# Gated-linear-attention level scores as 64x64 blocks in two column strips of TensorE

## The reference

```
b     = cumsum(logf)                                  # log decay within the chunk
inter = (q * exp(b)) @ S
att   = einsum('tk,sk,tsk->ts', q, k, exp(b_t - b_s))  for s <= t
intra = att @ v
S_new = exp(b_last) * S + (k * exp(b_last - b)).T @ v
o     = inter + intra
```

## Time and profile before

| | |
|---|---|
| median of 3 runs | 1457.23 us (1452.88, 1457.23, 1464.98) |
| profiled execution | span 1456.3 us; the page gives no other time of its own |
| PE busy | 1295.0 us, 89% of the span |
| VectorE busy | 727.9 us, 50% |
| ScalarE busy | 411.9 us, 28% |
| POOL busy | 173.9 us, 12% |
| L906, score matmuls, x384 | 49.8 us busy |
| L786, masked copies, x48 | 35.1 us busy |

### The profile page before, as it was taken

One profiled execution on the slowest core, in us unless ns is written; L12 is line 12 of the kernel. 1 busy time (PEld: TensorE's weight loads), 2 busy tenths in 40 slices (PEclk: granted clock), 3 DMA queues, 4 the chain that ended last, 5 costly groups with the idle time before them and its releaser, 6 DMA issues. The chain is left out here.

```text
span 1456.3 us, 29957 instructions
## 1 busy us (share of the span) xinstructions
PE 1295.0 (89%) x11855; PEld 763.7 (52%) x11855; DVE 727.9 (50%) x1882; ACT 411.9 (28%) x1100; POOL 173.9 (12%) x247
## 2 busy tenths in 40 slices
PE   6999999999799999876999989868778699998897
PEld 3445565556356665444555545445554355755452
DVE  4435777768655311137353544477885565321123
ACT  3023444544111211124213121234546211121112
POOL 2002233332011000003021100100100001000002
PEclk9999999999899899997999999988999799799998
DMA  6150437223804899995465899899999622899935
GB/s 235 59 152 2 122 88 222 76 79 133 292 35 156 330 374 349 322 331 195 145 232 216 331 338 375 330 405 378 408 404 365 224 99 90 333 366 340 351 84 195
DMA packets 133902, 348.15 MB, mean 239 GB/s; under 512 B 22603, under 2 KB 52478, under 8 KB 125566
## 3 DMA queue, kind: packets, MB, share of 16 engines
q1 hardware_dynamic: 115378, 311.53, 59.8%
q10 hardware_dynamic: 13388, 16.82, 3.5%
q0 software_dynamic: 4992, 17.83, 3.3%
HBM read 302.61 MB, written 43.52 MB: 238 GB/s over the span
## 5 line engine op out<-in xcount | busy, mean ns | idle before, releaser
L409 PE MATMUL bank<-wring,xT 128*128 128x512 f32 x448 | 199.6, 600 | 0.0
L409 PEld LDWEIGHTS bank<-wring,xT 128*128 128x128 f32 x448 | 83.9, 192 | 100.0 <-issue 99.9
L1443 PE MATMUL bank<-wring,xT 128*128 128x512 f32 x256 | 120.2, 623 | 2.0 <-DVE xT L1363 2.0
L886 PE MATMUL bank<-xT,wring 128*128 128x512 f32 x256 | 115.0, 608 | 3.9 <-DVE hgrn_g L708 3.9
L2812 DVE STREAM_TRANSPOSE attn_k_pages<-attn_k_pages 128x1024 f32<-128x1024 f32 x64 | 77.6, 1232 | 38.9 <-DMA attn_k_pages<-cache_k 38.4
L886 PEld LDWEIGHTS bank<-xT,wring 128*128 128x128 f32 x256 | 49.2, 194 | 66.2 <-issue 60.6
L1443 PEld LDWEIGHTS bank<-wring,xT 128*128 128x128 f32 x256 | 49.7, 201 | 60.1 <-issue 60.0
L2812 DVE STREAM_TRANSPOSE wring<-wring 128x1024 f32<-128x1024 f32 x44 | 52.7, 1223 | 47.0 <-DMA wring<-cache_k 47.0
L786 DVE COPY_PREDICATED gla_att<-level_masks,bank 128x512 f32<-128x512 int32 x48 | 35.1, 731 | 70.4 <-PE bank L906 70.4
L2321 PE MATMUL bank<-xT,wring 128*128 128x512 f32 x128 | 56.9, 597 | 0.0
L906 PE MATMUL bank<-gla_qe,gla_ke 128*128 128x128 f32 x384 | 49.8, 285 | 0.0
(11 more groups left out here) (461 smaller groups left out, 2388.2 us busy)
## 6 DMA issues: line engine op xcount, KB each, us to landing
attn_k_pages<-cache_k SPq DMA_DIRECT2D x64, 512.0 KB, 7.4
wring<-cache_v SPq DMA_DIRECT2D x56, 512.0 KB, 7.8
wring<-cache_k SPq DMA_DIRECT2D x44, 512.0 KB, 7.2
moe_wd<-moe_w_down SPq DMA_DIRECT2D x20, 1024.0 KB, 13.8
attn_shared<-cache_v SPq DMA_DIRECT2D x40, 512.0 KB, 5.7
wring<-moe_w_gate SPq DMA_DIRECT2D x18, 1024.0 KB, 11.9
wring<-moe_w_up SPq DMA_DIRECT2D x18, 1024.0 KB, 14.8
wring<-a_w_in SPq DMA_DIRECT2D x16, 1024.0 KB, 10.7
```

The costliest lines, as they stand in the source:

```text
L409: last = nc.tensor.matmul(bank[:, :], xT[:, c, cols(t)], w[:, c, :], start=(c == 0), stop=(c == DC - 1))
L886: last = nc.tensor.matmul(bank[:, :], lhsT, k.xT[:, c, 0:SEQ], start=(c == 0), stop=(c == DC - 1))
L1443: last = nc.tensor.matmul(bank[:, :], k.xT[:, c, cols(t)], w[:, c, :], start=(c == 0), stop=(c == DC - 1))
```

## The change

- Scores of a level are formed as blocks of 64 keys by 64 queries. For levels 0 to 4 only the two diagonal blocks of each chunk matter: 8 matmuls with 64 stationary and 64 moving columns, key block n in PSUM partitions 64n to 64n+63, so that the two of a chunk stand in two column strips of TensorE. For level 5 only the block of lower keys and upper queries is formed: 4 matmuls, all in the first strip. A head has 44 score matmuls in place of 24.
- Two levels share a bank (level 0 and 1 in bank 3, 2 and 3 in bank 4, 4 and 5 in bank 3 again), and `att_done` is raised once per two levels. PE waits once: before level 4, for levels 0 and 1 to be taken.
- DVE copies levels 0 to 4 by mask into a compact tile `gla_diagonals` (64 columns a chunk), and level 5 by a plain copy into its quarter of A.
- ACT copies the compact tile into the diagonal quarters of A (`diagonals_out`, two copies of 64 partitions); PE waits for it before A times v.
- QE[i] and KE[i] of levels 1 to 5 are one tile (queries in the upper halves, keys in the lower), and nothing of it is cleared. POOL makes the 64-column masks in the setup, 2 copies.

```diff
--- before.py
+++ after.py
@@ -37,6 +37,7 @@
 PAGE, PAGES = 128, 16
 PAST = PAGE * PAGES
 LEVELS = (8, 16, 32, 64, 128)
+BLOCK = P // 2
 LAM_INIT = 0.8 - 0.6 * math.exp(-0.3)
 FG_MIN = 2.0 ** -63
 MASKED = 1e30
@@ -245,6 +246,9 @@
         ch(nc.gpsimd.tensor_tensor(k.strip_sum[:, :], quarter(0), quarter(1), ALU.add))
         for j in range(2, 4):
             ch(nc.gpsimd.tensor_tensor(k.strip_sum[:, :], k.strip_sum[:, :], quarter(j), ALU.add))
+        for i in range(2):
+            part = slice(BLOCK * i, BLOCK * (i + 1))
+            ch(pool.tensor_copy(k.blockmask[part, :, :], k.levelmask[part, 0:len(LEVELS), part]))
         pool.sem_inc(self.tables_made, 1)
         k.order_n["gpsimd"] = ch.n
 
@@ -450,8 +454,10 @@
         diff = [sb(f"gla_diff{i}", [P, TOK]) for i in range(2)]
         inv4 = sb("gla_inv4", [P, TOK])
         eb, kd = sb("gla_eb", [P, TOK]), inv4
-        QE = [sb(f"gla_qe{i}", [P, TOK if i == 0 else SEQ]) for i in range(NLEV)]
-        KE = [sb(f"gla_ke{i}", [P, TOK if i == 0 else SEQ]) for i in range(NLEV)]
+        levels_qk = [sb(f"gla_qk{i}", [P, SEQ]) for i in range(1, NLEV)]
+        QE, KE = [sb("gla_qe", [P, TOK])] + levels_qk, [sb("gla_ke", [P, TOK])] + levels_qk
+        diagonals = sb("gla_diagonals", [P, PT, BLOCK])
+        k.blockmask = sb("block_masks", [P, len(LEVELS), BLOCK])
         smp_qf = sb("gla_sample_qf", [P, P])
         QS = sb("gla_qs", [P, TOK])
         QB = sb("gla_qb", [P, DEC_B * (SMP + DEC_T)])
@@ -508,7 +514,8 @@
         q_lev, k_lev = k.sem("q_level_ready"), k.sem("k_level_ready")
         kk_ready = k.sem("k_ready")
         turned, turned_out = k.sem("kd_turned"), k.sem("kd_turned_out")
-        att_done, att_taken = k.sem("att_done"), k.sem("att_taken")
+        att_done, att_taken, diagonal_out = k.sem("att_done"), k.sem("att_taken"), k.sem("att_diagonals_out")
+        ATT_GROUPS = NLEV // 2 + 1
         ds_done, s_ready = k.sem("state_step_done"), k.sem("state_ready")
         sds_done, sn_ready, sn_scaled = k.sem("sample_step_done"), k.sem("sample_state_ready"), k.sem("sample_state_scaled")
         vm_ready, o_done, o_out = k.sem("vm_ready"), k.sem("o_done"), k.sem("o_evacuated")
@@ -517,6 +524,7 @@
         s0_in = [k.sem(f"s0_landed{i}") for i in range(2)]
         s_store, sn_store = [k.sem("s_stored")], [k.sem("sn_stored")]
         head = lambda h: slice(h * P, (h + 1) * P)
+        level_part = lambda i, part: k.ps[3 + i // 2 % 2][part, (i % 2) * PT * BLOCK:(i % 2 + 1) * PT * BLOCK]
         blocks = lambda ap, n: ap.rearrange("p (c n) -> p c n", n=n)
         QBd = QB[:, :].rearrange("p (b x) -> p b x", x=SMP + DEC_T)[:, :, 0:DEC_T]
 
@@ -576,6 +584,13 @@
                     for i in range(2):
                         last = nc.scalar.activation(kdTs[halves[i], :], k.ps[6][0:SMP, P:2 * P], ACT.Copy)
                     last.then_inc(turned_out, 1)
+
+                def diagonals_out(h):
+                    act.wait_ge(att_taken, (NLEV + 1) * (h + 1) - 2)
+                    for i in range(2):
+                        part = slice(BLOCK * i, BLOCK * (i + 1))
+                        last = nc.scalar.activation(A[part, :, part], diagonals[part, :, :], ACT.Copy)
+                    last.then_inc(diagonal_out, 1)
 
                 def results(h):
                     act.wait_ge(o_done, h + 1)
@@ -609,6 +624,7 @@
                         for u in GATE_UNITS[h - 1]:
                             gate(u)
                         decays_turned(h - 1)
+                        diagonals_out(h - 1)
                     exponentials(h)
                     if h:
                         results(h - 1)
@@ -619,6 +635,7 @@
                 nc.scalar.activation(k.tmp, k.ms, ACT.Sqrt)
                 sum_taken(HEADS - 2)
                 decays_turned(HEADS - 1)
+                diagonals_out(HEADS - 1)
                 results(HEADS - 1)
                 squares(HEADS - 1)
                 sum_taken(HEADS - 1)
@@ -636,10 +653,6 @@
                     ch(nc.vector.tensor_scalar(lb[:, 1, :], lb[:, 1, :], 1.0, None, ALU.add))
                     ch(nc.vector.tensor_tensor(lb[:, 2, :], lb[:, 1, :], lb[:, 1, :], ALU.subtract))
                     ch(nc.vector.tensor_scalar(lb[:, 3, :], lb[:, 2, :], -1.0, 1.0, ALU.mult, ALU.add))
-
-                def clear_level(i):
-                    nc.vector.memset(QE[i + 1][:, :], 0.0)
-                    ch(nc.vector.memset(KE[i + 1][:, :], 0.0))
 
                 def clear_pads(x):
                     last = nc.vector.memset(g[32 * x:32 * x + 32, PT, :], 0.0)
@@ -677,18 +690,14 @@
                 bounds()
                 setup.lambda_sum(dve)
                 value_out(0, 2)
-                clear_level(0)
                 value_out(0, 3)
-                clear_level(1)
                 value_out(0, 4)
-                clear_level(2)
                 value_out(1, 0)
                 setup.lambda_out(dve)
-                clear_level(3)
-                clear_level(4)
                 value_out(1, 1)
                 nc.vector.memset(QB[:, :], 0.0)
                 nc.vector.memset(A[:, :, :], 0.0)
+                nc.vector.memset(diagonals[:, :, :], 0.0)
                 ch(nc.vector.memset(AS[:, :], 0.0))
                 clear_pads(1)
                 value_out(1, 2)
@@ -759,7 +768,7 @@
 
                         j = i - 1
                         if h and j == 0:
-                            dve.wait_ge(att_done, (NLEV + 1) * h)
+                            dve.wait_ge(att_done, ATT_GROUPS * h)
                             dve.wait_ge(o_done, h)
                         if j == 0:
                             dve.wait_ge(qf_out, 4 * h + 4)
@@ -781,12 +790,18 @@
                 def matrices(h):
                     if h:
                         dve.wait_ge(o_done, h)
+                        dve.wait_ge(diagonal_out, h)
                     for i in range(NLEV):
-                        dve.wait_ge(att_done, (NLEV + 1) * h + i + 1)
-                        nc.vector.copy_predicated(A[:, :, :], bcast(k.levelmask[:, i, :].bitcast(I32), 1, [P, PT, P]),
-                                                  k.ps[3 + i % 2][:, :].rearrange("p (c n) -> p c n", c=PT)).then_inc(att_taken, 1)
-                        dve.wait_ge(att_taken, (NLEV + 1) * h + i + 1)
-                    dve.wait_ge(att_done, (NLEV + 1) * (h + 1))
+                        dve.wait_ge(att_done, ATT_GROUPS * h + i // 2 + 1)
+                        src = level_part(i, slice(0, P)).rearrange("p (c n) -> p c n", c=PT)
+                        if i < NLEV - 1:
+                            ins = nc.vector.copy_predicated(diagonals[:, :, :], bcast(k.blockmask[:, i, :].bitcast(I32), 1, [P, PT, BLOCK]), src)
+                        else:
+                            ins = nc.vector.tensor_copy(A[0:BLOCK, :, BLOCK:P], src[0:BLOCK])
+                        ins.then_inc(att_taken, 1)
+                        if i < NLEV - 2:
+                            dve.wait_ge(att_taken, (NLEV + 1) * h + i + 1)
+                    dve.wait_ge(att_done, ATT_GROUPS * (h + 1))
                     nc.vector.copy_predicated(AS[:, :], k.levelmask[0:SMP, 0, 0:SMP].bitcast(I32), k.ps[7][0:SMP, 0:SMP])\
                         .then_inc(att_taken, 1)
                     if h + 1 < HEADS:
@@ -835,7 +850,7 @@
                 for h in range(HEADS):
                     ebase = (NLEV + 3) * h
                     if h:
-                        pool.wait_ge(att_done, (NLEV + 1) * h)
+                        pool.wait_ge(att_done, ATT_GROUPS * h)
                     for j in range(NLEV):
                         pool.wait_ge(exp_ready, ebase + (2 if j == 0 else 3 + j))
                         if j == 0:
@@ -899,12 +914,15 @@
                         nc.tensor.transpose(k.ps[5][:, c * P:(c + 1) * P], kd[:, c * P:(c + 1) * P], k.ident[:, :])
                     nc.tensor.transpose(k.ps[6][0:SMP, P:2 * P], kd[:, SEQ:TOK], k.ident[:, :]).then_inc(turned, 1)
                     for i in range(NLEV):
-                        if i >= 2:
-                            pe.wait_ge(att_taken, (NLEV + 1) * h + i - 1)
+                        if i == NLEV - 2:
+                            pe.wait_ge(att_taken, (NLEV + 1) * h + 2)
                         for c in range(PT):
-                            part = slice(c * P, (c + 1) * P)
-                            last = nc.tensor.matmul(k.ps[3 + i % 2][:, part], KE[i][:, part], QE[i][:, part], start=True, stop=True)
-                        last.then_inc(att_done, 1)
+                            at = [slice(c * P + BLOCK * n, c * P + BLOCK * (n + 1)) for n in range(2)]
+                            for n in range(2 if i < NLEV - 1 else 1):
+                                out = level_part(i, slice(BLOCK * n, BLOCK * (n + 1)))[:, c * BLOCK:(c + 1) * BLOCK]
+                                last = nc.tensor.matmul(out, KE[i][:, at[n]], QE[i][:, at[n if i < NLEV - 1 else 1]], start=True, stop=True)
+                        if i % 2:
```

(2 more changed lines are left out.)

## The result

| | before | after |
|---|---|---|
| median | 1460.09 us (4 runs, 1452.88 to 1464.98) | 1444.8 us (4 runs, 1443.32 to 1446.61) |
| profiled span | 1456.3 | 1442.1 |
| end of the last head | 366.9 | 344.4 |
| the rest of the span | 1089.4 | 1097.7 |

The ratio is 0.9871, 95% interval 0.9826 to 0.9916. A repetition gave 0.9855 (0.9802 to 0.9908). The change is faster by 15.3 us in the medians, 22.0 were predicted. In this pair of profiles the heads gained 22.5 us, and 8.3 of it are missing behind them. "Heads" is the recurrence of the 8 heads, up to its last state matmul; "the rest" is all of the span behind it.

A forecast was written before the change was run, and what follows sets the result against it. PE's list was taken to bound six heads, the chain heads 6 and 7. 8 heads x 2.8 = 22.4 us, less 0.4 for Ln, off the 1456.3 span gave 1434.3; plus 0.9 to the median, 1435.2 us, range 1427 to 1449.

The forecast's parts named there:

- What bounds: In the heads, six are bound by PE's list, heads 6 and 7 just by the chain ending in POOL's `gla_inv`.
- Matmuls at 0.029: Score block on PE: 0.028 to 0.030 us for each of 80 instructions, 0.056 for the 8 of level 5.
- The rival without overlap: Score block: loads do not overlap between strips, 88 x 0.056 = 4.9 us on PE, total 1450; chance 0.10.
- Masked copy 0.44, plain copy 0.42: DVE in the score block: a masked copy of 256 columns takes 0.44 us, level 5's plain copy 0.42.
- The new wait of PE: In the score block, before level 4, PE waits for level 1 to be taken and loses about 0.2 us.
- ACT: Compact-tile copies over by 4.8 us, Ln from 6.1, scan at 7.0 with 0.2 us left; costed at nothing.
- both rivals: Clock at 0.50 in heads: after each block, 1447, chance 0.08; through the rest of each head's block, 1500, chance 0.03.
- The heads: Recurrence of 8 heads: each 2.8 us shorter by the score block, 22.4 us in all.
- The stage behind moves as a whole: Behind the heads: the next stage starts its loads after a barrier and stays as long as it was; no cost.
- Faster than 1442.6: Whole kernel: a time below 1442.6 us, beyond the 14.6 us a measurement can tell from no change; chance 0.78.

The follow-up runs named there:

- serial order: The change with the score loops turned, per level first the four blocks of one strip, then the four of the other; median 1445.8 us.
- direct copies: The change without compact tile and ACT copies, VectorE copying levels 0 to 4 by mask straight into A, two copies per level; median 1461.1 us.
- thrice-made copies: The change with each of ACT's two copies of the compact tile made three times, the additional ones into a spare tile; median 1447.6 us.
- third bank: The change with levels 4 and 5 in bank 7 and the sample scores in bank 6; median 1439.6 us.
- short delay of two matmuls: The change with two 128x512 matmuls, result unread, on TensorE behind the last head; median 1446.4 us.

## Why the prediction was right, and where it was not

- **What bounds**: right in the main. Both lists shortened by the block. PE's wait for `gla_inv` stayed at 1.9 us once, as predicted (2). One reading was off: the copies did hold PE up a little before. In head 0 the 48 instructions start 112 ns apart, not 126, save at six places, which cost 0.5 us in all, and the weight loads of the scores waited 2.5 us for the copies over the heads. With the change they wait 2.6 us, so this wait was not new.
- **Matmuls at 0.029**: right. In a block the instructions start in pairs, one for each strip, 58 to 59 ns apart; level 5, in one strip, has 58 ns per instruction (0.056 predicted). The rival without overlap (4.9 us) is refuted by the 3.3 to 3.4 us of the block on PE, its wait included. The serial order supports this from another side. The Trainium skill's rule that weight loads overlap with matmuls only in another row group ("TensorE: Matmul & The Clock Gate", Part 3, The mechanism) does not hold here as that list puts it: both strips used all 128 rows. The same section also lets a load run ahead into a background weight buffer; whether that is what happens here, no run shows.
- **Masked copy 0.44, plain copy 0.42**: measured 0.446 and 0.406. That the width counts and the partitions do not was shown by the direct copies.
- **The new wait of PE**: taken as 0.2, it is 0.32 to 0.41 between the starts on either side of it, because DVE starts 1.20 after the first score and not 1.1. The block was thus 4.62 and not 4.4, and the saving 2.6 to 2.8 a head in place of 2.8, save in head 6.
- **ACT**: copies over at 4.76 (4.8), Ln at 6.07 (6.1), scan at 6.97 (7.0). No cost, as said, with the cover used up; the thrice-made copies show that it was.
- **The clock in the heads**: both rivals failed in the form in which they were put, a fall in each head or in most. No block of the change ran at the lower level in its own two profiles. But one block can: that of head 6 did in the third bank's profile and in that of the change with a short delay of two matmuls, and it cost 1.5 and 1.1 us there.
- **The heads**: 22.5 us, predicted 22.4, and this agreement is luck. Seven heads gained 2.6 to 2.8 in the block; head 6 gained 4.0 (8.61 to 4.62), because its block before ran at the lower level and did not in the change's profile. With 2.63 a head it would be 21. The profile of the change with the delay of two matmuls, where head 6's block runs at the lower level as before, shows it: from the first score to the end of the heads it takes 212.3 us, 21.2 less than the 233.6 of before.
- **"The stage behind moves as a whole"**: this is the step that failed, and the term that was mis-sized. It was priced at 0 and is about +5 us on average (1098.6 against 1093.4), so the saving is 17.3 us on average in place of 22.0. The scatter of these stages, 1084 to 1106 us in the 65 runs of the kernel before, was given "a few us" in the range and nothing in the sum, though the three runs shown lay 12 us apart.
- **The total**: 1444.8 lies in the range 1427 to 1449, but 9.6 above the forecast's 1435.2. Half of that is the saving (22.0 for 17.3). The other half is the starting point: the three runs gave a median of 1457.2, the 65 runs have a mean of 1462.0. The range was wide for the sake of rivals that did not come true, and it is by this that the result lies in it. Faster than 1442.6, held to be likely with 0.78, it was not.

What makes the 5 us is open. The runs speak against the start of the later stages and, by the direct copies, against the scores or the tiles alone. The rest goes with the time at 1.2 GHz (10 us more of it, 3.7 us by the slope), but which brings the other about is not shown. By the profiles most of the scatter is in the attention stage: 438 us in the first profile of before and 448 in the second (granted clock 0.96 and 0.94), 443 and 445 with the change (0.94 and 0.93). Why PE should spend more time at the lower level behind a change that ends before these stages was not found. Part of the 5 us could also be a typical heads' end other than the profiles', as said above the table.

## What to carry to other kernels

Halving the stationary and the moving columns of small matmuls and spreading them over two strips pays on TensorE by the full factor of the columns (a level went from 8 instructions 112 ns apart to 16 that take 29 ns each), but only if the engine that empties the banks also gets less to do; its copies go by columns and not by partitions, so pack both strips into one copy. Count the block on every list that contains it; if all shorten alike, the saving goes through. Before a stage's saving is booked on the total, look at how much the stages behind it differ from run to run, and compare the clock of the two profiles head by head before an agreement is called one.

## What was not expected of the hardware

- Matmuls of two column strips overlap even if four of one strip stand before four of the other: the block is 5.11 us in place of 4.62, not 6.3.
- A masked copy of 64 partitions by 256 columns takes 442 ns, one of 128 partitions 446.
- The same kernel with the same instructions spends 1084 to 1106 us in the same stages, on one core (65 runs, worked out with the heads' end of two profiles); from the first score to the end of the heads two profiles of each kernel agree within 0.1 us (233.6 and 211.2).
- With two additional waits of about 1 us in each head (direct copies) the granted clock was 0.50 in three stretches within the heads, and with the change in none.
